# Squares of the last output tile: summed by VectorE into the running tile, or by TensorE on their own

## The reference

```python
def rmsnorm(x, g):
    y = xf * lax.rsqrt(jnp.mean(xf * xf, axis=-1, keepdims=True) + EPS)
    return (y * g)
for l in range(DEPTH):                                       # DEPTH = 2
    h = rmsnorm(x, g_mix[l]) * (1.0 + sc_a) + sh_a
    z = h @ w_in[l] + b_in[l]
    ...                                                      # gated convolution, sparse attention
    x = x + ga_a * (mixed_in @ w_o[l])
    h = rmsnorm(x, g_mlp[l]) * (1.0 + sc_m) + sh_m
    x = x + ga_m * (jnp.square(jax.nn.relu(h @ w_ff1[l])) @ w_ff2[l])
return rmsnorm(x, g_final)
```

## Time and profile before

| | us |
|---|---|
| median of 3 runs (3386.69 to 3388.49) | 3387.36 |
| the profiled execution | 3386.8 |
| its span | 3385.0 |
| TensorE busy (PE) | 3240.5, 96% |
| VectorE busy (DVE) | 1612.0, 48% |
| GpSimd busy (POOL) | 1338.4, 40% |
| ScalarE busy (ACT) | 787.6, 23% |

### The profile page before, as it was taken

The page is one execution under the profiler, slowest core; times in us unless marked ns, Lnnn a source line. Parts: engine busy times, 40 slices in busy tenths (PEclk is TensorE's granted clock), DMA queues, the critical chain, the costliest instruction groups (busy, mean ns, idle before and its releaser), DMA issues.

```text
span 3385.0 us, 38776 instructions
## 1 busy us (share of the span) xinstructions
PE 3240.5 (96%) x15455; PEld 2643.7 (78%) x15485; DVE 1612.0 (48%) x2087; ACT 787.6 (23%) x1331; POOL 1338.4 (40%) x1327
## 2 busy tenths in 40 slices
PE   5999998998899999999999999989979999999999
PEld 4888886676688888888878888867658888888887
DVE  6643245887546433232375333568764532222224
ACT  2100113666212000000120001256751310000002
POOL 2433331333464444444444333313334644444443
PEclk7999999999999999999999999999989999999999
DMA  6434631000522221111143355200015211111112
GB/s 230 133 106 131 187 80 33 1 1 1 193 75 88 75 72 54 50 50 50 50 145 99 113 154 152 59 16 1 1 38 175 75 45 50 50 50 48 46 50 81
DMA packets 293371, 263.02 MB, mean 78 GB/s; under 512 B 10315, under 2 KB 273735, under 8 KB 292680
## 3 DMA queue, kind: packets, MB, share of 16 engines
q1 hardware_dynamic: 278354, 206.61, 20.6%
q10 hardware_dynamic: 14838, 53.94, 4.2%
HBM read 222.76 MB, written 30.41 MB: 75 GB/s over the span
## 4 chain that ended last, share of the span: by engine, by line
PE 88%; DVE 7%; ACT 2%; issue 2%; POOL 0%; ACTq 0%; DVEq 0%; POOLq 0%
PE lin L1045 75%; PE aux L1255 2%; DVE pTL L1839 2%; PE pv L1269 2%; DVE negm L1833 2%; PE lin L1231 1%; PE pv L1270 1%; PE lin L1232 1%; PE pv L1120 1%; PE lin L1210 1%; ACT pTH L1522 1%; PE lin L1065 1%; PE lin L1066 1%; PE lin L1067 1%; DVE acc L835 1%
## 5 line engine op out<-in xcount | busy, mean ns | idle before, releaser
L1016 POOL TENSOR_SCALAR whi<-wraw 128x512 fp32r<-128x512 f32 x504 | 411.1, 816 | 1511.0 <-PE lin L1045 1430.4
L1018 POOL TENSOR_TENSOR wlo<-wraw,whi 128x512 fp32r<-128x512 f32 x504 | 739.2, 1467 | 42.1
L1045 PE MATMUL lin<-hH,whi 128*128 128x512 f32 x2176 | 674.7, 391 | 0.0
L1045 PE MATMUL lin<-hL,whi 128*128 128x512 f32 x2176 | 671.2, 390 | 0.0
L1045 PE MATMUL lin<-hH,wlo 128*128 128x512 f32 x2176 | 670.8, 389 | 0.0
L1045 PEld LDWEIGHTS lin<-hH,wlo 128*128 128x128 f32 x2176 | 408.7, 188 | 86.0
L1045 PEld LDWEIGHTS lin<-hL,whi 128*128 128x128 f32 x2176 | 408.7, 188 | 85.5
L1045 PEld LDWEIGHTS lin<-hH,whi 128*128 128x128 f32 x2176 | 405.9, 188 | 82.6 <-issue 0.8
L1886 DVE SCALAR_TENSOR_TENSOR xT<-lin,adac,xT 128x1024 f32<-128x1024 f32 (+1 forms) x164 | 189.2, 1154 | 525.1 <-PE lin L1045 524.2
L996 POOL TENSOR_SCALAR prob<-prob,fac 128x640 f32<-128x640 f32 (+7 forms) x256 | 184.5, 721 | 466.9 <-DVE fac L1823 448.9
L1921 DVE TENSOR_TENSOR tmp<-tmp 128x1024 f32<-128x1024 f32 x64 | 137.2, 2143 | 432.1 <-ACT tmp L1576 431.9
(11 more groups left out here) (249 smaller groups left out, 3902.6 us busy)
## 6 DMA issues: line engine op xcount, KB each, us to landing
wraw<-in_w_ff SPq DMA_DIRECT2D x134, 512.0 KB, 3.8
wraw<-in_w_ada SPq DMA_DIRECT2D x80, 512.0 KB, 3.8
wraw<-in_w_in SPq DMA_DIRECT2D x78, 512.0 KB, 5.1
wraw<-in_w_o SPq DMA_DIRECT2D x24, 512.0 KB, 3.7
adar<-in_w_ada SPq DMA_DIRECT2D x16, 512.0 KB, 11.2
x_keep<-xT ACTq DMA_DIRECT2D x4, 2048.0 KB, 8.9
mix_keep<-tmp ACTq DMA_DIRECT2D x16, 512.0 KB, 3.5
gate_keep<-ropes ACTq DMA_DIRECT2D x16, 512.0 KB, 6.6
```

Source lines behind the costliest of these rows:

```text
L1016: pool.tensor_scalar(high, raw, 1.0, 1.0, ALU.mult, ALU.mult).then_inc(w_hi, 1)
L1018: pool.tensor_tensor(wlo[:, SLOT[n], hf], raw, high.bitcast(F32), ALU.subtract).then_inc(w_split, 1)
L1045: mm = pe.matmul(lin[c % 2][:, hf], w, m(k)[:, hf], start=first, stop=last)
```

## The change

The last tile's squares are added by VectorE too (`add_squares` for i = 7, once for each half), and TensorE sums `tmp[:, 0]` alone, after the wait for that sum.

```diff
@@ piece_counts
-            if 0 < i < KC - 1:
+            if i:
                 ss[n, i, h] = len(ss) + 1
@@ sum_squares (TensorE)
-        def sum_squares(pe, n, h, between=None):
-            sums_of = lambda t: aux[:, 512 + t:512 + t + 1]
-            pe.wait_ge(ss_added, SS_NO[n, KC - 2, h])
+        def sum_squares(pe, n, h):
+            pe.wait_ge(ss_added, SS_NO[n, KC - 1, h])
             for t in range(4 * h, 4 * h + 4):
-                pe.matmul(sums_of(t), tmp[:, 0, t * P:(t + 1) * P], ones[:, 0:1],
-                          start=t % 4 == 0, stop=False, skip_group_check=True)
-            if between:
-                between()
-            pe.wait_ge(sq_made, SQ_NO[n, KC - 1, h])
-            for t in range(4 * h, 4 * h + 4):
-                mm = pe.matmul(sums_of(t), tmp[:, 1, t * P:(t + 1) * P], ones[:, 0:1],
-                               start=False, stop=t % 4 == 3, skip_group_check=True)
+                mm = pe.matmul(aux[:, 512 + t:512 + t + 1], tmp[:, 0, t * P:(t + 1) * P], ones[:, 0:1],
+                               start=t % 4 == 0, stop=t % 4 == 3, skip_group_check=True)
             mm.then_inc(ss_done, 1)
@@ add_squares (VectorE)
-            if 0 < i < KC - 1:
+            if i > 0:
                 dve.wait_ge(sq_made, SQ_NO[n, i, h])
                 dve.tensor_tensor(tmp[:, 0, cut(h)], tmp[:, 0, cut(h)], tmp[:, 1, cut(h)], ALU.add).then_inc(ss_added, 1)
                 dve.wait_ge(ss_added, SS_NO[n, i, h])
@@ vector program, n1 (norms 1 and 3)
                     residual(("wo", i, 0), 2 * KC, i, X_NO[n1, i, 0], 0)
+                add_squares(dve, n1, KC - 1, 0)
                 for i in range(FULL[1], KC):
...
                     norm_chunks(dve, n1, 0, *SCALED_BETWEEN[1][i])
+                add_squares(dve, n1, KC - 1, 1)
                 norm_mean(dve, n1, 1)
@@ vector program, n2 (norms 2 and 4)
                     residual(("f2", NFG - 1, i, 0), 5 * KC, i, X_NO[n2, i, 0], 0)
+                add_squares(dve, n2, KC - 1, 0)
                 for i in range(FULL[0], KC):
...
+                add_squares(dve, n2, KC - 1, 1)
                 if n2 == LAST:
-                    dve.wait_ge(sq_made, SQ_NO[LAST, KC - 1, 1])
                     dve.tensor_scalar(xT[:, KC - 1, half[1]], xT[:, KC - 1, half[1]], g_fin(KC - 1), None, ALU.mult).then_inc(f_v, 1)
                 norm_mean(dve, n2, 1)
```

## The result

| | before | after |
|---|---|---|
| median, 22 runs each | 3388.51 | 3394.73 |
| lowest to highest | 3386.33 to 3391.18 | 3391.96 to 3397.98 |
| profiled execution | 3386.8 | 3396.95 |
| its span | 3385.0 | 3395.1 |

The change made the kernel slower by 6.2 us: ratio 1.0019, 95% interval 1.0012 to 1.0025. The prediction was 3390.2, a loss of 2.8 us that a measurement could hardly tell from nothing; what came is the place and the mechanism of its rival A, priced at +7.2.

What follows compares the result with a forecast made beforehand. TensorE, busy 96% of the span, was taken as the bound. Half 0 -2.3, half 1 of norms 1 and 3 +1.6, norm 2 +2.4 and +0.4, end +0.7: +2.8 us, forecast 3390.2, range 3386.8 to 3394.5.

Steps and rivals of the forecast that it cites:

- rival A: Clock also falls behind half 1 of norms 1 and 3: 1.7 us each, +7.2 in all, 3394.6; chance 0.10.
- The price of a set: At each of eight sums, one set fewer shortens TensorE's work by 0.80 us, 6.4 if nothing waits.
- the add: VectorE's add takes 0.69 us, or ends 0.54 after a running GpSimd split; TensorE starts 0.05 later.
- Half 0: Norms 1 to 4: the add is held by a split, yet each place gains 0.58 us, 2.3 in all.
- Half 1 of norms 1 and 3, the wait: TensorE waits for square and add, product 0.81 us later at each place, 1.6 lost in all.
- Half 1 of norms 1 and 3, the clock: Behind these two sums TensorE's clock stays at 1.00, so no loss was counted.
- Half 1 of norm 2: VectorE is late: 2.4 us lost waiting, TensorE idle 5.0, plus 0.4 for the low clock.
- The end: Half 1 of norm 4: sum and transposes come later by 0.7 us, all of it showing.
- The range: Whole kernel: 3386.8 to 3394.5, meant to hold the forecast and reach just short of the +7.2 case.

Runs made afterwards that it cites:

- fill_waits: Changed kernel with unread 384-column matmuls ahead of TensorE's wait at half 1 of norms 1 to 3: 3389.70 against 3387.66 before, ratio 1.0008.
- half0_only: Kernel before, with the new add and single set only in half 0 of norms 1 to 4: 3386.24 against 3387.66, ratio 0.9996.
- half1_only: Kernel before, with the new add and single set only in half 1 of norms 1 to 4: 3397.85 against 3387.66, ratio 1.0031.
- later_sum: Changed kernel with half 1's sum in `opening` behind the whole first product, spread later too: 3385.06 against 3387.66 before, ratio 0.9992.
- its repeat: The changed kernel with later sum and spread in `opening`, measured a second time: 3384.10 against 3388.51 before, ratio 0.9989.
- n13_half1: Kernel before, with the new add and single set only in half 1 of norms 1 and 3: 3393.07 against 3388.41, ratio 1.0015.
- end_half1: Kernel before, with the new add and single set only in half 1 of norm 4, the end: 3388.93 against 3388.51, ratio 1.0002.
- later_end_old: Changed kernel with later sum and spread in `opening`, but the old two sets in half 1 of norm 4: 3383.36 against 3388.51 before, ratio 0.9985.
- add_ahead_n2: Changed kernel, but norm 2's half 1 add stands ahead of the last normalized tile: 3392.91 against 3388.41 before, ratio 1.0013.
- n2_half1: Kernel before, with the new add and single set only in half 1 of norm 2: 3390.88 against 3388.41, ratio 1.0010.

## Why the prediction was wrong, point by point

- **The price of a set** (0.80 to 0.90) and **the add** (0.54 behind the split, 0.05 to TensorE): right. The profile after has 0.71 at norm 1, 1.17 beside a split, 0.68 and 0.69 without, and gains of 0.56 and 0.57 where 0.58 was forecast. By the Trainium skill ("SBUF — State Buffer", section "Who interferes with whom") the shared port pair is an exclusive lock; a full hold of 0.69 behind a split would have made the gains 0.43, and the measurement decides for the shorter one.
- **Half 0**: four gains, 2.3 us forecast, 2.3 by the profiles; alone they measured 1.4, with an interval from 4.1 faster to 1.7 slower.
- **Half 1 of norms 1 and 3, the wait**: 0.81 each forecast, 0.81 and 0.82 measured. The set that was taken away had lain beside ScalarE's square, and the add went onto the path.
- **Half 1 of norms 1 and 3, the clock: the step that failed.** The prediction took the clock behind these sums to stay at 1.00 and has no term for it in its sum, "against it: the 2.2 us gap with the clock still at 1.00". Measured: 0.50 for 3.4 us at each, 1.61 us behind the sum at norm 1, 1.55 by fill_waits, 3.2 us in all. That is nearly the whole of what the forecast lacked: 2.8 + 3.2 = 6.0. Norm 2 adds 0.5 (below), which makes 6.5, against 6.2 measured.

The row that I took for evidence shows one execution, and a gap with full products on both sides of it, no one-column ones. The same 2.2 us gap at norm 2, which no edit touches, is followed by a low stretch of 3.4 us in 8 of the 13 profiles at hand (after, half0_only, half1_only, later_sum and its repeat, n13_half1, end_half1, later_end_old) and by none in the other 5. So it spoke neither for nor against. These are single executions of different kernels; what tells the 8 from the 5 is not shown. Behind the new wait at norms 1 and 3, with the sum's records following it, the clock was low at all 8 places of the 4 profiles that have it (after, half1_only, n13_half1, add_ahead_n2), and at none of the others. Each time it fell 0.9 to 1.8 us after the sum's start; these are four executions, so not eight independent cases.
- **Half 1 of norm 2**: 2.8 forecast in all (2.4 wait, 0.4 clock); 3.3 to 3.6 by the profiles, 2.5 by the median of n2_half1. The wait was right: in n2_half1 5.03 us of idle, 5.0 forecast. The sum's own records at the low clock were mis-sized, 0.3 forecast and 0.8 measured (1.86 instead of 1.05). The products up to the spread cost 0.1 more than before, as forecast.
- **The end**: 0.7 forecast, 0.73 by the profile.
- **The range** ended at 3394.5, "just short of A"; the median came out at 3394.73. Rival A had the right place, and its price, 1.7 a place, was right to 0.15. Its total of +7.2 also held 1.0 more at norm 2, of which about half came. It was given 0.10 on the strength of one row.

The Trainium skill's rule on the clock ("TensorE: Matmul & The Clock Gate", "What's actually happening": throttled by default, released by activity) points the same way as the rows of norms 1 and 3: the clock behind the wait is 1.00 where TensorE was kept busy during it, 0.50 where it wasn't.

## What to carry to other kernels

Fewer instructions on the bounding engine gain only where that engine would not otherwise be waiting; ask of each instruction that you take away what it lies beside, place by place. A new wait on TensorE is to be priced with its wake: here a wait that cost 0.8 us drew a stretch at half clock that cost 1.6 more. When a reading decides between two cases, look whether it is the same in several executions; and if the result is needed later anyway, move its consumer behind independent matmuls before moving work to another engine.

## What the runs showed of the hardware

- A wait of 1.45 us with eight one-column matmul records behind it was followed by 3.4 us at 0.50 in 8 of 8 places; the two sets back to back without a wait, 1.7 us of one-column records, by no such stretch (norms 1 and 3 of before, half0_only, n2_half1 and end_half1).
- With 384-column matmuls during the wait (fill_waits, norms 1 and 3) the clock stayed at 1.00, though the wait's end and the sum were the same.
- At the low clock the eight records of a sum took 1.67 to 1.87 us instead of 1.05.
- A gap of 2.24 us, the same in every profile, was followed by the low clock in 8 of 13. In the old form that stretch cost 0.5 us and not 1.4 to the spread, since TensorE then waited less for the add (0.38 instead of 1.20). This, and 1.5 us ahead of norm 1 and 1.3 in the attention, are differences between two single executions that the change has no part in; the 22 runs spread over 4.9 us before and 6.0 us after. Which share of that spread is the clock's, and what decides it each time, stays open.
